# Two passes over each weight block: sixteen matmuls on the rounded weights, then sixteen on their rests

## The chip, the cores and the metric

The kernel runs on one core of a Trainium2 chip. The metric is the device time of that core in microseconds (us): 3598.67 us, the median of 3 runs (3596.43 to 3601.0). TensorE is the matmul engine; its granted clock is 1.2 or 2.4 GHz (0.50 or 1.00 in the profile's shares). VectorE (DVE) and ScalarE (ACT) do the elementwise work, SyncE (SP) issues the DMAs that bring the weights, GpSimd (POOL) does almost nothing.

## The reference, cut to what matters

The model is four layers on 256 tokens of width 2048, in float32: a windowed attention layer and a gated linear recurrence layer, each followed by a convolutional feed-forward part, and then an "even" and an "odd" attention layer. Almost all the work is dense projections of this kind:

```python
def conv_ffn(h, w_up, conv_w, conv_b, w_down):
    u = causal_dwconv(h @ w_up, conv_w, conv_b)
    g, v = jnp.split(u, 2, axis=-1)
    return (jax.nn.gelu(g, approximate=True) * v) @ w_down

# first_block: for layer in range(2):
#     x = x + sliding_window_attention(rmsnorm(x, ...), w_qkv, ..., w_o)   (layer 0)
#     x = x + rglru_block(rmsnorm(x, ...), w_in, ..., w_out)               (layer 1)
#     x = x + conv_ffn(rmsnorm(x, ...), w_up, ..., w_down)                 (D_FF = 6144)
# then an even layer (grouped-query heads with rotary positions, then differential heads)
# and an odd layer (16 dilated-window heads), each: x = x + (gated heads) @ w_out
```

## The kernel before, in words

Everything is kept transposed: features on the 128 partitions, the 256 tokens along the free axis. A *block* (a "unit" in the code) is one tile of 128 output features: its weights are 16 k-tiles of 128x128, held in one slot of 128x2048. There are 540 blocks, streamed in a fixed order of phases (table PHASES): `attn` 24 (the QKV projection), `wo` 16, three rounds of `up` 32 and `down` 16, `lru_y` 16, `lru_x` 32 (16 of them small gate blocks), `lru_out` 16, three more rounds of `up` and `down`, `even_kv` 4, `even_a` 16, `even_b` 32, `even_out` 16, `odd` 64, `odd_out` 16.

The float32 product is split in two float32r parts. ScalarE rounds the raw weights (`w_head`, L561), VectorE subtracts to get the rest (`w_tail`, L837). Activations are split the same way and stand side by side, 256 rounded columns and 256 of rests, in `h` (layer input) or `act` (input of the second product). For each k-tile TensorE runs one 128x512 matmul of `w_head` on both halves (L272) and one 128x256 matmul of `w_tail` on the rounded half (L273). All 32 matmuls of a block add up in one PSUM bank: columns 0 to 255 hold head times rounded plus tail times rounded, columns 256 to 511 head times rests. Two banks alternate.

Each engine has its own written order, joined by semaphores. For a block ScalarE first rounds the weights of the block three ahead (L561), then copies columns 256 to 511 (`lo`, L567) once `unit_done` says that the last matmul is through; VectorE adds columns 0 to 255 to it (`prod`, L843), scales it, makes the rest of the weights three ahead (L837) and does the phase's own work. TensorE may start a block when its weights are split (`tail_done`) and the bank of two blocks ago is read (`bank_free`).

Two arguments of `unit` put waits inside a block. `ready` is given to the first block of a phase whose input is just being made: before k-tile 0 it waits for the first 14 input tiles, before k-tile 14 for the fifteenth and before k-tile 15 for the last. `middle` is a list of small pieces issued after k-tile 8 (k == KT // 2): in the projection the column sums of a head's norm (`head_norm`, L289), in `even_kv` and `even_a` also rotations (`rotate`, L297), transposes of values (`turn_v`, L307), scores (L315), transposes of probabilities (`turn_p`, L326) and values (L335); in `even_b` and `odd` scores after k-tile 8 of the first block of four, `turn_p` in the third and the values in the fourth. Each piece begins with its own wait, and TensorE works strictly in order behind it. After the first block of a normed phase stands `token_norm` (L283), which waits for the sum of squares (`acc_done`). The very first block (`first_unit`, L373, L374) and the gate blocks (`gate_unit`, L430 to L432: twelve 128x256 matmuls in a row, each with its own weights) are written apart.

Of the kernel before, what the change touches and what calls it, by code (L numbers as in the profile page):

```python
# [29 lines left out]
P = 128  # L30
D_MODEL, SEQ = 2048, 256
KT = D_MODEL // P
# [53 lines left out]
def known(v):  # L86
    return isinstance(v, int)
# [30 lines left out]
def build(nc, t):  # L118

    ctx = ExitStack()  # L120
    with ctx:
        def sb(name, shape, dt=F32):
            return ctx.enter_context(nc.sbuf_tensor(name, shape, dt))
# [9 lines left out]
        w_tail = sb("w_tail", [P, RING, D_MODEL], F32R)  # L133
# [125 lines left out]
        def _(pe):  # L259
            def unit(u, slot, src, middle=(), ready=None):  # L260

                bank = unit_bank[slot % 2]
                pe.wait_ge(tail_done, u + 1)
                if not known(u) or u >= 2:
                    pe.wait_ge(bank_free, u - 1)
                for k in range(KT):
                    if ready and k in (0, KT - 2, KT - 1):
                        pe.wait_ge(ready[0], ready[1] - (2 if k == 0 else KT - 1 - k))  # L270
                    at = slice(k * P, (k + 1) * P)
                    pe.matmul(bank[:, :], w_head[:, slot, at], src[:, k, :], start=k == 0, stop=False)  # L272
                    last = pe.matmul(bank[:, 0:SEQ], w_tail[:, slot, at], src[:, k, 0:SEQ],  # L273
                                     start=False, stop=k == KT - 1)
                    if k == KT // 2:
                        for part in middle:
                            part()
                last.then_inc(unit_done, 1)

            def token_norm(n):  # L280
# [58 lines left out]
            def plain(name, src, ready=None, norm=None):  # L339

                def body(i):
                    for j in range(RING):
                        first = known(i) and j == 0
                        unit(i * RING + (BASE[name] + j), j, src, ready=ready if first else None)
                        if first and norm is not None:
                            token_norm(norm)
                repeat(pe, 0, UNITS[name] // RING, body)
# [40 lines left out]
            def project(i):  # L388
                for j in range(RING):
                    g = i * RING + j  # L390
                    if known(g) and g == 0:
                        first_unit()
                    else:
                        unit(i * RING + (BASE["attn"] + j), j, h, (trailing(i * RING + (j - 1)),))
# [41 lines left out]
            for j in range(2):  # L436
                unit(b + j, j, h)
# [23 lines left out]
            for i in range(A_HEADS // 2 + 1):  # L461

                n, last = 2 * i - 2, i == A_HEADS // 2
# [920 lines left out]
```

## Time and profile before

| | |
|---|---|
| median of 3 runs | 3598.67 us |
| profiled execution, device time | 3606.35 us |
| its span, first to last instruction | 3604.6 us |
| mean granted TensorE clock | 0.943 |
| TensorE matmul (PE) busy | 3336.0 us, 93% |
| TensorE weight load (PEld) busy | 2820.0 us, 78% |
| VectorE busy | 2456.4 us, 68% |
| ScalarE busy | 1789.5 us, 50% |
| head matmuls L272 | 5808 on `h`, 2560 on `act` |
| tail matmuls L273 | 5808 on `h`, 2560 on `act` |

The profile is of one execution, and durations below are its own. Matmuls overlap in the pipeline: a single one is shown with 0.40 or 0.28 us although the next starts earlier, so what a matmul costs is read from the distance between two starts. A bracket at the end of a row gives the idle time of that engine ahead of the instruction and who ended it. The chain of waits is followed backwards from the last instruction.

### The profile page before, as it was taken

What the parts mean: (1) busy time and instruction counts of PE and PEld (TensorE: products, weight loads), DVE (VectorE), ACT (ScalarE), POOL (GpSimd) and SP (SyncE); (2) the same over time, 40 slices, a digit from 0 to 9 for tenths busy, and PEclk for the clock granted to TensorE, in tenths of its full rate; (3) what the DMA queues carried; (4) which work ended last, traced back from release to release, by engine and by line L of the source; (5) the groups of instructions that cost most, each with busy time, mean ns of one, the idle gap of its engine ahead of it and who ended that gap; (6) DMA issues with size and microseconds to landing.
All of it is one profiled execution on the core that took longest, in us unless ns stands there. A gap on an engine that the chain in (4) does not pass through costs nothing.

```text
span 3604.6 us, 52426 instructions
## 1 busy us (share of the span) xinstructions
PE 3336.0 (93%) x17960; PEld 2820.0 (78%) x17960; DVE 2456.4 (68%) x3703; ACT 1789.5 (50%) x2281; POOL 13.1 (0%) x20
## 2 busy tenths in 40 slices
PE   8878999999999999769999999999778989999997
PEld 6744788888888888658888888888666777888876
DVE  6654577667667766777875775776455776666665
ACT  6843355445445445664554554554444554444443
POOL 1000000000000000000000000000000000000000
PEclk9965899999999999879999999999888999999998
DMA  5410355555555554235555555555223444445443
GB/s 186 144 43 0 105 186 187 181 187 184 182 187 186 182 180 150 95 117 176 197 186 187 186 179 186 185 184 186 105 84 105 152 149 141 174 164 175 173 146 122
DMA packets 83038, 561.11 MB, mean 156 GB/s; under 512 B 9728, under 2 KB 12800, under 8 KB 15872
## 3 DMA queue, kind: packets, MB, share of 16 engines
q1 hardware_dynamic: 82944, 559.87, 44.7%
q8 instruction: 57, 0.93, 0.1%
q14 instruction: 37, 0.30, 0.0%
HBM read 557.73 MB, written 2.10 MB: 155 GB/s over the span
## 4 chain that ended last, share of the span: by engine, by line
PE 70%; DVE 14%; issue 6%; ACT 6%; DMA 3%; DVEq 1%; ACTq 0%; SPq 0%
PE unit L272 42%; PE unit L273 21%; DVE w_tail L837 5%; PE o L335 2%; PE s L315 2%; PE tr L326 1%; DVE prod L843 1%; ACT w_head L561 1%; ACT L576 1%; DMA raw<-in_down 1%; ACT lo L567 1%; DMA raw<-in_lru_x 1%; ACT prt L613 1%; DVE mx L885 1%; DVE x L1024 0%
## 5 line engine op out<-in xcount | busy, mean ns | idle before, releaser
L272 PE MATMUL unit<-h,w_head 128*128 128x512 f32 x5808 | 2108.4, 406 | 40.1 <-DVE kv L1100 33.7
L273 PE MATMUL unit<-h,w_tail 128*128 128x256 f32 x5808 | 1643.3, 283 | 0.0
L272 PEld LDWEIGHTS unit<-h,w_head 128*128 128x128 f32 x5808 | 1110.9, 191 | 319.3 <-DVE kv L1100 37.0
L561 ACT ACTIVATE w_head<-raw 128x2048 fp32r<-128x2048 f32 (+1 forms) x540 | 1013.5, 1877 | 611.3 <-DMA raw<-in_up 210.8
L837 DVE TENSOR_TENSOR w_tail<-raw,w_head 128x2048 fp32r<-128x2048 f32 (+1 forms) x540 | 1209.5, 2240 | 11.5
L273 PEld LDWEIGHTS unit<-h,w_tail 128*128 128x128 f32 x5808 | 1115.4, 192 | 3.0
L272 PE MATMUL unit<-act,w_head 128*128 128x512 f32 x2560 | 910.7, 400 | 19.1 <-DVE act L854 12.9
L843 DVE TENSOR_TENSOR prod<-unit,lo 128x256 f32<-128x256 f32 x524 | 222.3, 424 | 756.2 <-ACT lo L567 750.4
L273 PE MATMUL unit<-act,w_tail 128*128 128x256 f32 x2560 | 720.6, 281 | 0.0
L272 PEld LDWEIGHTS unit<-act,w_head 128*128 128x128 f32 x2560 | 485.2, 190 | 140.6 <-DVE act L854 15.2
L273 PEld LDWEIGHTS unit<-act,w_tail 128*128 128x128 f32 x2560 | 487.7, 190 | 0.2
L567 ACT ACTIVATE lo<-unit 128x256 f32<-128x256 f32 x524 | 197.2, 376 | 316.2 <-PE unit L273 315.8
L691 ACT ACTIVATE kv<-kv,fconv 128x256 f32<-128x256 f32 x192 | 115.8, 603 | 187.3 <-DVE kv L849 187.3
L1045 DVE SCALAR_TENSOR_TENSOR kv<-kv,fconv 128x255 f32<-128x255 f32 (+1 forms) x384 | 184.8, 481 | 24.8 <-DVE kv L1045 0.9
L613 ACT ACTIVATE prt<-tr 128x512 f32<-128x512 f32 x64 | 38.3, 598 | 188.3 <-PE tr L326 188.3
L326 PE MATMUL tr<-ident,pr 128*128 128x128 f32 x256 | 59.4, 375 | 54.1 <-DVE pr L900 35.8
L607 ACT ACTIVATE pr<-pr,nm 128x256 f32<-128x256 f32 x144 | 71.5, 498 | 74.5 <-DVE nm L887 74.5
L849 DVE SCALAR_TENSOR_TENSOR kv<-prod,rstd 128x256 f32<-128x256 f32 x232 | 98.6, 425 | 9.0
L326 PEld LDWEIGHTS tr<-ident,pr 128*128 128x128 f32 x256 | 39.4, 188 | 82.5 <-DVE pr L900 41.5
L335 PE MATMUL o<-prt,kv 128*64 128x256 f32 (+1 forms) x160 | 72.3, 601 | 23.4 <-ACT prt L613 23.4
L587 ACT ACTIVATE sq<-x 128x256 f32 (+1 forms) x96 | 40.3, 419 | 107.9 <-DVE x L1024 107.9
L315 PE MATMUL s<-kv,store 64*128 64x256 f32 (+1 forms) x160 | 73.8, 622 | 9.9 <-DVE store L986 5.2
(157 smaller groups left out, 1610.4 us busy)
## 6 DMA issues: line engine op xcount, KB each, us to landing
raw<-in_up SPq DMA_DIRECT2D x192, 1024.0 KB, 4.9
raw<-in_down SPq DMA_DIRECT2D x96, 1024.0 KB, 4.9
raw<-in_odd SPq DMA_DIRECT2D x64, 1024.0 KB, 4.9
raw<-in_even_b SPq DMA_DIRECT2D x32, 1024.0 KB, 4.9
raw<-in_attn SPq DMA_DIRECT2D x24, 1024.0 KB, 4.9
raw<-in_wo SPq DMA_DIRECT2D x16, 1024.0 KB, 4.9
raw<-in_lru_y SPq DMA_DIRECT2D x16, 1024.0 KB, 4.9
raw<-in_lru_x SPq DMA_DIRECT2D x16, 1024.0 KB, 4.9
```

The source lines that it names most:

```text
L272: pe.matmul(bank[:, :], w_head[:, slot, at], src[:, k, :], start=k == 0, stop=False)
L273: last = pe.matmul(bank[:, 0:SEQ], w_tail[:, slot, at], src[:, k, 0:SEQ], start=False, stop=k == KT - 1)
L315: last = pe.matmul(bank[:, qt * SEQ:(qt + 1) * SEQ], q[:, qt * P:(qt + 1) * P], k, start=True, stop=True)
L326: last = pe.transpose(ps_t[:, kt * SEQ + qt * P:kt * SEQ + (qt + 1) * P], pr[:, slot, qt * SEQ + kt * P:qt * SEQ + (kt + 1) * P], ident[:, :])
L335: last = pe.matmul(out, v[kt], prt[:, kt * SEQ:(kt + 1) * SEQ], start=kt == 0, stop=kt == QT - 1)
L561: a.activation(w_head[:, slot, 0:width], raw[:, r, 0:width], ACT.Copy).then_inc(head_done, 1)
L567: a.activation(lo[:, slot % 2, :], unit_bank[slot % 2][:, SEQ:2 * SEQ], ACT.Copy).then_inc(lo_done, 1)
L691: a.activation(kv[:, 1 + j, :], kv[:, 0, :], ACT.Identity, scale=fconv[:, layer, tap, 2:3], bias=fconv[:, layer, tap, 3:4])\
L837: v.tensor_tensor(w_tail[:, slot, 0:width], raw[:, slot % 2, 0:width], w_head[:, slot, 0:width].bitcast(F32), ALU.subtract).then_inc(tail_ ...
L843: v.tensor_tensor(prod[:, :], unit_bank[slot % 2][:, 0:SEQ], lo[:, slot % 2, :], ALU.add)\
L849: return v.scalar_tensor_tensor(dst, prod[:, :], scale, rstd[:, :], ALU.mult, ALU.mult)
L1045: ins = v.scalar_tensor_tensor(y[:, back_by:SEQ], kv[:, 0, 0:SEQ - back_by], w, y[:, back_by:SEQ], ALU.mult, ALU.add)
```

## The change

The loop over the 16 k-tiles is split in two. The first loop issues the 16 head matmuls, with the waits of `ready` and the pieces of `middle` at the same k-tiles as before; a second loop issues the 16 tail matmuls. The first matmul of a block still clears the bank, the last tail still closes the sum and signals `unit_done`. `first_unit` and `gate_unit` are not touched.

```diff
@@ -270,11 +270,12 @@
                         pe.wait_ge(ready[0], ready[1] - (2 if k == 0 else KT - 1 - k))
                     at = slice(k * P, (k + 1) * P)
                     pe.matmul(bank[:, :], w_head[:, slot, at], src[:, k, :], start=k == 0, stop=False)
-                    last = pe.matmul(bank[:, 0:SEQ], w_tail[:, slot, at], src[:, k, 0:SEQ],
-                                     start=False, stop=k == KT - 1)
                     if k == KT // 2:
                         for part in middle:
                             part()
+                for k in range(KT):
+                    last = pe.matmul(bank[:, 0:SEQ], w_tail[:, slot, k * P:(k + 1) * P], src[:, k, 0:SEQ],
+                                     start=False, stop=k == KT - 1)
                 last.then_inc(unit_done, 1)
```

TensorE's order at the end of the first block of a `down` phase, before. The waits on `act_done` are those for the last two tiles of `act`:

```order
L272 MATMUL unit<-act,w_head 128x512
L273 MATMUL unit<-act,w_tail 128x256
L272 MATMUL unit<-act,w_head 128x512 [waits act_done]
L273 MATMUL unit<-act,w_tail 128x256
L272 MATMUL unit<-act,w_head 128x512 [waits act_done]
L273 MATMUL unit<-act,w_tail 128x256
L272 MATMUL unit<-act,w_head 128x512 [waits bank_free,tail_done]
```

The same block after the change, from its first matmul to the next block's:

```order
L272 MATMUL unit<-act,w_head 128x512 [waits act_done,bank_free,tail_done]
L272 MATMUL unit<-act,w_head 128x512 x13
L272 MATMUL unit<-act,w_head 128x512 [waits act_done] x2
L277 MATMUL unit<-act,w_tail 128x256 x16
L272 MATMUL unit<-act,w_head 128x512 [waits bank_free,tail_done]
```

Ahead of the last wait stood 15 heads and 15 tails, and now 15 heads; behind it stood one head and one tail, and now one head and 16 tails.

TensorE's order around k-tile 8 of the fourth block of a group in `even_a`, before (`o` is a head's values, `v` the rotation of the second query head):

```order
L272 MATMUL unit<-h,w_head 128x512
L273 MATMUL unit<-h,w_tail 128x256
L335 MATMUL o<-prt,kv 128x256 [waits o_read,pt_done]
L335 MATMUL o<-prt,kv 128x256
L297 MATMUL v<-store 128x256 [waits vt_done,q_done,rot_in]
L272 MATMUL unit<-h,w_head 128x512
L273 MATMUL unit<-h,w_tail 128x256
```

And the whole block after the change:

```order
L272 MATMUL unit<-h,w_head 128x512 [waits bank_free,tail_done]
L272 MATMUL unit<-h,w_head 128x512 x8
L336 MATMUL o<-prt,kv 128x256 [waits o_read,pt_done]
L336 MATMUL o<-prt,kv 128x256
L298 MATMUL v<-store 128x256 [waits vt_done,q_done,rot_in]
L272 MATMUL unit<-h,w_head 128x512 x7
L277 MATMUL unit<-h,w_tail 128x256 x16
```

The pieces stood after nine heads and nine tails, and now after nine heads; behind them stood seven heads and seven tails, and now seven heads and 16 tails.

## Rows read from the trace of the kernel before

**Rows 1.** The page, parts 1, 4 and 5: busy time, chain, costliest groups.

```profile
PE 3336.0 (93%) x17960; PEld 2820.0 (78%) x17960; DVE 2456.4 (68%) x3703; ACT 1789.5 (50%) x2281; POOL 13.1 (0%) x20
...
PE 70%; DVE 14%; issue 6%; ACT 6%; DMA 3%; DVEq 1%; ACTq 0%; SPq 0%
...
L272 PE MATMUL unit<-act,w_head 128*128 128x512 f32 x2560 | 910.7, 400 | 19.1 <-DVE act L854 12.9
```

**Rows 2.** Stretches: length, then busy us and instructions of each engine, clock, DMA.

```profile
670.00:930.00 260.00, 260.00 (x1474) 225.42 (x1473) 185.09 (x244) 128.56 (x137) 0.00 (x0) 1.00 0.53 185
1700.00:1870.00 170.00, 170.00 (x983) 148.59 (x982) 139.47 (x204) 97.61 (x112) 0.00 (x0) 1.00 0.55 191
```

**Rows 3.** Timeline, TensorE, first down phase: start, length, instruction, idle before.

```profile
666.88 0.28 PE L273 MATMUL unit<-act,w_tail 128*128 128x256 f32 x1
668.03 0.50 PE L272 MATMUL unit<-act,w_head 128*128 128x512 f32 x1 [0.88 <-DVE act L854]
```

**Rows 4.** Timeline, TensorE, first block of lru_y and its norm.

```profile
1302.83 0.50 PE L272 MATMUL unit<-h,w_head 128*128 128x512 f32 x1 [0.74 <-DVE h L860]
...
1305.36 1.22 PE L283 MATMUL norm<-acc,ones 128*128 128x256 f32 x2 [1.92 <-DVE acc L869]
```

**Rows 5.** Timeline, TensorE, a gate block: matmuls, and a weight load.

```profile
1465.19 0.28 PE L430 MATMUL unit<-act,w_head 128*128 x1
1465.31 0.28 PE L431 MATMUL unit<-act,w_head 128*128 x1
...
1465.19 0.19 PEld L431 LDWEIGHTS unit<-act,w_head 128*128 128x128 f32 x1
```

**Rows 6.** Timeline, TensorE, a down phase, slow rhythm.

```profile
1000.71 0.40 PE L272 MATMUL unit<-act,w_head 128*128 128x512 f32 x1
1000.95 0.28 PE L273 MATMUL unit<-act,w_tail 128*128 128x256 f32 x1
1001.07 0.40 PE L272 MATMUL unit<-act,w_head 128*128 128x512 f32 x1
```

**Rows 7.** Timeline, TensorE, an up phase, fast rhythm.

```profile
1750.04 0.27 PE L273 MATMUL unit<-h,w_tail 128*128 128x256 f32 x1
1750.15 0.40 PE L272 MATMUL unit<-h,w_head 128*128 128x512 f32 x1
1750.38 0.28 PE L273 MATMUL unit<-h,w_tail 128*128 128x256 f32 x1
```

**Rows 8.** A stretch and the timeline, TensorE and ScalarE, end of an even_a block.

```profile
2637.20:2641.80 4.60, 4.60 (x16) 3.83 (x15) 0.85 (x3) 0.00 (x0) 0.00 (x0) 0.50 0.07 25
...
2641.34 0.63 PE L272 MATMUL unit<-h,w_head 128*128 128x512 f32 x1
2641.77 0.41 PE L273 MATMUL unit<-h,w_tail 128*128 128x256 f32 x1
...
2642.22 0.38 ACT L567 ACTIVATE lo<-unit 128x256 f32<-128x256 f32 x1 [8.99 <-PE unit L273]
```

**Rows 9.** Timeline, start of even_out, and VectorE's last act tile.

```profile
2986.08 0.99 PE L272 MATMUL unit<-act,w_head 128*128 128x512 f32 x1
...
2991.41 0.43 DVE L854 TENSOR_TENSOR act<-store,act 128x256 fp32r<-128x256 f32 x1
```

**Rows 10.** Timeline, projection: next block's first matmul, and ScalarE's copy.

```profile
134.31 0.40 PE L272 MATMUL unit<-h,w_head 128*128 128x512 f32 x1
...
136.53 0.36 ACT L567 ACTIVATE lo<-unit 128x256 f32<-128x256 f32 x1
```

**Rows 11.** Timeline, TensorE, even_b, third block of four.

```profile
2872.11 0.65 PE L326 MATMUL tr<-ident,pr 128*128 128x128 f32 x4 [1.42 <-DVE pr L914]
```

**Rows 12.** Timeline, VectorE and TensorE, odd, third block of four.

```profile
3192.77 0.62 DVE L900 TENSOR_SCALAR pr<-pr,rd 128x256 f32<-128x256 f32 x2
...
3194.62 0.60 PE L326 MATMUL tr<-ident,pr 128*128 128x128 f32 x4
```

**Rows 13.** Line L567 from 2520 to 2740: who ended ScalarE's idle time.

```profile
  PE unit L273: 45.7, 8
```

## The prediction

> **What bounds the kernel now.** I read the page first: TensorE is busy 93% of the span, and the chain that ended last lies 70% on it and 14% on VectorE [rows 1]. Then the stretches of the span. In the feed-forward stages TensorE never stops and the granted clock is 1.00 (2.4 GHz): 260 us hold 1474 matmuls, which is 737 pairs of one 512-column matmul on a rounded block (head) and one 256-column matmul on its rest (tail), so 352.8 ns a pair; another stretch of 170 us holds 983 matmuls, 491.5 pairs, 345.9 ns each [rows 2]. So the same code runs at two rhythms. Of the 385 blocks that nothing interrupts 303 go in the slow rhythm and 82 in the fast one (counted by the starts of their first matmuls), a mean of 351.3 ns a pair. 432 of the 523 blocks that the change touches stand in stages bound by this rhythm (288 feed-forward, 80 of the five other plain stages of 16 [wo, lru_y, lru_out, even_out, odd_out], 64 odd attention): 6912 pairs, so 1 ns a pair is 6.9 us of the kernel.
>
> Then the waits, since the change moves the places in a block where TensorE waits. There are three kinds. (a) The first block of a phase waits for the last activation tile before k-tile 15: TensorE stood from 666.88 to 668.03 [rows 3], and the page charges 12.9 us of such waiting to the tile's writer on the line of the act blocks [rows 1]. (b) The first block of a normed phase waits the same way and is then followed by a norm matmul that waits for the sum [rows 4]. (c) In the attention stages small work is issued after k-tile 8 and waits for VectorE or ScalarE.
>
> **The change part by part.** It removes nothing and adds nothing: 16 head and 16 tail matmuls with their 32 weight loads stand in each block as before; only their order differs. No DMA, no other engine and no semaphore changes. What moves is what is late.
>
> *The rhythm.* In a run of heads and a run of tails each kind follows itself. Tails have a row: in the gate blocks 256-column matmuls follow each other, each with its own weights, at 0.12 us [rows 5]; in the alternation a head starts 0.11 or 0.12 after a tail [rows 6, 7]. Heads after heads have no row. A tail starts 0.23 to 0.24 us after a head [rows 6, 7], and that is the nearest I have for the time that a head holds the array: 241 ns at most. Below, the fast rhythm less a 120 ns tail leaves 226 ns, and, farther off, half of the 0.43 us that a head takes at the lower clock (0.50 granted, 1.2 GHz) is 213 ns [rows 8]. So a pair in two passes costs 226 + 120 = 346 to 241 + 120 = 361 ns, against 351.3. The tail's 120 is measured, four more than the 116 it has in the slow rhythm. If the cost above the columns' own time belongs to each matmul and its load and is only booked on the neighbour, the order does not matter. I take that, 352 ns, a change of 0; the ends are -5.3 x 6.9 = -37 us and +9.7 x 6.9 = +67 us.
>
> The Trainium skill, "TensorE: Matmul & The Clock Gate", section "Back-to-back issue gap", gives N/2.4 + 2.5 ns as the isolated gap of a matmul of N columns at full clock. That would be 216 + 109 = 325 ns a pair in either order; the trace shows 346 to 353 [rows 2], so the rule lacks some 20 to 28 ns here and cannot say whose they are. By it the rhythm term would be 0, as an estimate, if the excess stays, and far below 0 if alternation makes it.
>
> *The last tile of a phase.* Before, 15 heads and 15 tails are done when TensorE waits for the last act tile, and after it one head and one tail remain. Now only the heads are done, and 15 tails more remain: 15 x 0.12 = 1.8 us later at each such place. The wait only starts earlier, since VectorE makes the tile from the last up block, whose end does not move. There are seven such places, the six down phases and lru_out (of the 12.9 us the six take 0.88 each [rows 3], the rest is lru_out's). At that one the lower clock makes the tails 0.21 us each at first, but the clock would rise no later than before, so in the end only columns at full clock are lost: 1.8. Sum 7 x 1.8 = 12.6 us, all on the path, since TensorE is the bound behind it. The other boundaries are free: at wo and odd_out the tile comes early in the block, and even_out's is there at 2991.84, 5.8 us after the block's start, while fifteen heads at the lower clock need up to 15 x 0.43 = 6.4 [rows 9].
>
> *Normed phases.* The last h tile came at 1302.83 and the norm matmul could start at 1305.36 [rows 4]. The two-pass block needs 0.24 + 16 x 0.12 = 2.16 us from there and ends at 1304.99: hidden, 0.37 us to spare. The same at the five such places. If that cover went, each would cost up to 1.8 us.
>
> *Work after k-tile 8.* Its place moves from 9 pairs (3.2 us) into the block to 9 heads (2.1 us); behind it stand 7 heads and 16 tails instead of 7 pairs: 9 x 0.12 = 1.08 us more. Where TensorE waits there for another engine, the block's end moves by that much against the work after k-tile 8. It costs only if somebody waits for that end.
> - QKV projection: the block ends at 134.31 and ScalarE takes it up at 136.53, because it makes roots and rounds weights until then [rows 10]. 2.2 us of cover against 1.08: 0. Its entry may shift by some 0.7.
> - Differential attention (even_b): the turn of the probabilities waits for VectorE [rows 11]; the block ends 1.6 us or more before ScalarE comes for it. 0. Its first scores can come up to 0.7 earlier, which cancels the entry above.
> - Odd attention: VectorE ends the probabilities at 3193.39, TensorE turns them at 3194.62 without a wait [rows 12]. This place would move 1.08 earlier against the block's end, and 1.23 of slack takes it: 0. If that failed, 16 x 1 us.
> - even_kv and even_a: eight times ScalarE stood idle until the block's last matmul, 45.7 us in all [rows 13]. One of them: last tail issued at 2641.77, ScalarE takes the block up at 2642.22 [rows 8]. Each of the eight costs 9 tails, 1.08 us at full clock, 9 x 0.21 = 1.9 where the lower clock lasts. Together 8.6 to 15; I take 10, since the low stretch usually ends within a microsecond of the block's end.
>
> **Sum:** 12.6 + 10 + 0 = +22.6 us on the profiled execution's 3606.35 us (span 3604.6): 3629. That execution stands 7.7 us above the median of the runs, 3598.67, so the median would be 3621.3. What a measurement can tell from no change is 0.2%, 7.2 us.
>
> **Rivals.**
> 1. *Runs of one kind go faster, and the kernel with them* (the other side). A load starts together with the matmul before it (1465.19 for both [rows 5]), so each head covers its successor's load twice over. If heads in a row then take 226 ns, a pair is 346 and the rhythm gives -37 against +22.6: 3584. It decides from a pair of 348.0 ns down (22.6 / 6.9 = 3.3 under 351.3). For it: the fast rhythm exists, unexplained, for the same instructions. Against: the gate blocks' tails are at the slow end of the tail intervals. Its extreme, 213 + 120 = 333, gives 3598.7 + 22.6 - 126 = 3495.
> 2. *Short after short is bound by the weight load.* In alternation a tail's slot was 112 to 117 at times, in its own run always 120; if heads keep the slow rhythm's 237, a pair is 357: +5.7 x 6.9 = +39, in all 3660; with 241, 3688. For it: [rows 5] against [rows 7]. Against: the 4 ns may be the head's, booked one matmul later.
> 3. *The moved waits cost nothing and the rhythm stays:* each later end is caught up by slack that I read as none: 3600. Against it: after such a wait TensorE has no idle time for 260 us in which 1.8 us could be won back [rows 2].
>
> The Trainium skill, same page, Part 2 step 1 ("Step-by-step"), says that the queue pulls weight loads ahead of running matmuls, so with two loads ahead one long matmul could shelter both its neighbour's and the next, which the two-pass order would lose. The trace shows a load never starting before the matmul ahead of it (1465.19 for both [rows 5]), so only one load is ahead and no shelter is lost; with two ahead it would come out as rival 2.
>
> **How the numbers follow.** Forecast case (waits as summed, rhythm within 2 ns): 0.47, 3607 to 3640. Rival 1: 0.24 (its extreme 0.03 of it). Rival 2: 0.19. Rival 3: 0.10. The time is the likeliest case's, 3621. The range goes down to rival 1's 3584 with a little room and up into rival 2, 3576 to 3662; its own range for the forecast case is 3607 to 3640. Faster by over 0.2%: rival 1 without its border cases, 0.22. Within 0.2%: most of rival 3 and rival 1's border, 0.11. Slower: 0.67.
>
> **What would show it.** Right: the head to head interval near 0.23 and the tail to tail near 0.12 in the feed-forward stages, 16 of each in 5.63 us; at a down phase the last act tile followed by one head and 16 tails, 2.2 us; the norm matmul of a normed phase still waiting for its sum, not for the block; eight blocks of even_kv and even_a ending 1.1 to 1.9 us later after their middle work. Wrong: a count of pairs in 260 us other than about 737; TensorE waiting in the odd attention at the turn of the probabilities; or ScalarE's wait for block ends turning up in the projection.

## The result and the profile after

The two-pass kernel takes 3614.82 us (median of 7 runs, 3609.33 to 3621.56) where the kernel before took 3599.32 us in its 7 (3596.43 to 3607.44). The ratio of the runs is 1.004, with a 95% interval of 1.0028 to 1.0052: 0.4% slower, 15 us. The forecast was 3621, slower.

The page of the two-pass kernel, parts 1, 4 and 5; columns as in [rows 1]:

```profile
PE 3330.3 (92%) x17960; PEld 2846.2 (79%) x17960; DVE 2454.5 (68%) x3703; ACT 1786.0 (49%) x2281; POOL 13.1 (0%) x20
...
PE 72%; DVE 12%; issue 6%; ACT 6%; DMA 3%; DVEq 1%; ACTq 0%; SPq 0%
...
L272 PE MATMUL unit<-act,w_head 128*128 128x512 f32 x2560 | 626.6, 397 | 32.0 <-DVE act L855 25.8
```

As many instructions as before, and the idle time that the last act tiles end has doubled, from 12.9 to 25.8 us. The stretches answer to [rows 2]; two lie inside feed-forward stages, the third behind the first of those waits:

```profile
1890.00:2140.00 250.00, 250.00 (x1439) 220.97 (x1439) 178.96 (x236) 123.95 (x134) 0.00 (x0) 1.00 0.54 188
1710.00:1870.00 160.00, 160.00 (x918) 141.23 (x918) 131.87 (x190) 90.42 (x105) 0.00 (x0) 1.00 0.55 190
670.10:674.00 3.90, 3.90 (x17) 3.81 (x18) 0.00 (x0) 0.00 (x0) 0.00 (x0) 0.50 0.40 170
```

250 us hold 719.5 pairs, 347.5 ns each, and the fast stretch of before is slightly slower now, 348.6. A stretch cuts its first and last block (this one holds 464 heads and 454 tails), so whole phases are the better measure: the 512 pairs of up01 take 178.13 us, 347.9 ns each, where they took 180.91, 353.3 ns, in the slow rhythm and 177.49, 346.7 ns, in the fast one (in e5 below). There is one rhythm: of the 380 blocks that nothing interrupts 376 take 5.57 us from end to end, where before 303 took 5.65 and 82 took 5.55. So where TensorE is bound by its own work the new order is faster than the slow rhythm, and slightly slower than the fast one. The third stretch shows the clock at 0.50. TensorE's timeline at the same place as [rows 3], where equal matmuls in a row are drawn together (x15, x16):

```profile
661.75 2.08 PE L277 MATMUL unit<-h,w_tail 128*128 128x256 f32 x16
663.66 3.59 PE L272 MATMUL unit<-act,w_head 128*128 128x512 f32 x15
670.01 0.79 PE L272 MATMUL unit<-act,w_head 128*128 128x512 f32 x1 [2.76 <-DVE act L855]
670.60 3.62 PE L277 MATMUL unit<-act,w_tail 128*128 128x256 f32 x16
674.02 2.27 PE L272 MATMUL unit<-act,w_head 128*128 128x512 f32 x5
```

The last act tile comes 6.35 us after the block began, as before (6.34). TensorE waits 2.76 us for it instead of 0.88, and behind it stand one head and 16 tails, which at 1.2 GHz take 4.0 us (670.01 to 674.02) where 2.16 was forecast and a pair took 0.47 before.

The boundary of lru_y, answering to [rows 4]:

```profile
1310.04 0.50 PE L272 MATMUL unit<-h,w_head 128*128 128x512 f32 x1 [1.89 <-DVE h L861]
1310.38 3.14 PE L277 MATMUL unit<-h,w_tail 128*128 128x256 f32 x16
1313.32 1.05 PE L284 MATMUL norm<-acc,ones 128*128 128x256 f32 x2
```

The norm matmul no longer waits for its sum (no bracket): it waits for the block's own tails. It starts 3.28 us after the last h tile, 2.53 before, and the clock is low for most of the way (the stretch: busy us and matmuls of TensorE, clock, DMA):

```profile
1310.40:1313.30 2.90, 2.90 (x17) 0.60 0.26 110
```

And the idle time of ScalarE that a block's last matmul ends, from 2520 to 2760, which holds the same 20 blocks as [rows 13]:

```profile
  PE unit L277: 54.1, 10
```

The span by phases, in us, each phase from the sum (`prod`) of the last block of the phase ahead of it to its own (read from the traces of this kernel, of the one before and of four experiments told below):

| phases | before | two passes | e1 | e3 | e4 | e8 |
|---|---|---|---|---|---|---|
| attn and wo | 481.1 | 484.6 | 481.9 | 480.3 | 482.1 | 484.2 |
| up01, up02, up11, up12, each | 180.9 | 178.1 | 178.3 | 178.2 | 178.1 | 178.1 |
| down00, 01, 10, 11, mean | 91.6 | 93.9 | 90.3 | 90.3 | 92.1 | 95.1 |
| down02 and down12 | 187.8 | 195.7 | 188.2 | 188.3 | 192.3 | 198.5 |
| up00, lru_y and up10 | 452.5 | 448.8 | 446.4 | 447.9 | 448.7 | 454.9 |
| lru_x and lru_out | 299.8 | 300.9 | 299.3 | 299.6 | 301.7 | 303.8 |
| even_kv and even_a | 223.5 | 232.0 | 233.3 | 223.6 | 231.2 | 243.5 |
| even_b to the end | 869.7 | 869.8 | 867.4 | 866.5 | 866.8 | 869.3 |
| span | 3604.6 | 3619.8 | 3590.8 | 3580.1 | 3603.8 | 3647.2 |

The four up phases that have no boundary with a wait win 2.8 us each. The six down phases lose 17 us net, 25 against the rhythm (16 blocks win 1.4 us in each), and the two even phases lose 8.5.

### The profile page after: what moved, and what is told of

Same layout as the page of the kernel before. It is cut to its first block, busy times and chain, and to the rows that moved or that the text cites. A ratio compares the mean times of both kernels' runs of the same rounds, so it can differ in the third digit from the quotient of the medians.

```text
span 3619.8 us, 52426 instructions
## 1 busy us (share of the span) xinstructions
PE 3330.3 (92%) x17960; PEld 2846.2 (79%) x17960; DVE 2454.5 (68%) x3703; ACT 1786.0 (49%) x2281; POOL 13.1 (0%) x20
## 4 chain that ended last, share of the span: by engine, by line
PE 72%; DVE 12%; issue 6%; ACT 6%; DMA 3%; DVEq 1%; ACTq 0%; SPq 0%
PE unit L272 42%; PE unit L277 23%; DVE w_tail L838 4%; PE o L336 2%; PE s L316 2%; PE tr L327 2%; DVE prod L844 1%; ACT L577 1%; ACT w_head L562 1%; ACT lo L568 1%; DMA raw<-in_lru_x 1%; ACT prt L614 1%; DMA raw<-in_wo 1%; DMA raw<-in_down 1%; DVE x L1025 0%
## 5 line engine op out<-in xcount | busy, mean ns | idle before, releaser
L272 PE MATMUL unit<-h,w_head 128*128 128x512 f32 x5808 | 1470.6, 403 | 44.1 <-DVE kv L1101 30.9
L272 PEld LDWEIGHTS unit<-h,w_head 128*128 128x128 f32 x5808 | 1094.7, 193 | 267.3 <-DVE kv L1101 33.5
L838 DVE TENSOR_TENSOR w_tail<-raw,w_head 128x2048 fp32r<-128x2048 f32 (+1 forms) x540 | 1209.4, 2240 | 11.5
L277 PEld LDWEIGHTS unit<-h,w_tail 128*128 128x128 f32 x5808 | 754.3, 193 | 30.8
L277 PE MATMUL unit<-h,w_tail 128*128 128x256 f32 x5808 | 761.1, 284 | 0.0
L272 PE MATMUL unit<-act,w_head 128*128 128x512 f32 x2560 | 626.6, 397 | 32.0 <-DVE act L855 25.8
L277 PEld LDWEIGHTS unit<-act,w_tail 128*128 128x128 f32 x2560 | 335.8, 195 | 12.4
L277 PE MATMUL unit<-act,w_tail 128*128 128x256 f32 x2560 | 339.5, 287 | 0.0
```

The lines of the kernel that those rows point to most:

```text
L277: last = pe.matmul(bank[:, 0:SEQ], w_tail[:, slot, k * P:(k + 1) * P], src[:, k, 0:SEQ], start=False, stop=k == KT - 1)
L838: v.tensor_tensor(w_tail[:, slot, 0:width], raw[:, slot % 2, 0:width], w_head[:, slot, 0:width].bitcast(F32), ALU.subtract).then_inc(tail_ ...
```

## The experiments

All of these are edits of the two-pass kernel's loop in `unit`, but e5. The diffs are shortened at the dots, and their comments are added here. The ratios are to runs of the kernel before that were taken together with them: medians 3596.68 (29 runs, for e1 to e4) and 3598.28 us (23 runs, for e5 to e8). The cuts in e1, e2, e3, e6 and e7 are the k-tiles at which a run of heads ends and their tails follow.

**e1, the first block of each phase back in the alternating order.**

```diff
-for k in range(KT):
+cuts = list(range(1, KT + 1)) if ready else [KT]
+k0 = 0
+for k1 in cuts:
+    for k in range(k0, k1):
...
         pe.matmul(bank[:, :], w_head[:, slot, k * P:(k + 1) * P], src[:, k, :], start=k == 0, stop=False)
...
+    for k in range(k0, k1):
         last = pe.matmul(bank[:, 0:SEQ], w_tail[:, slot, k * P:(k + 1) * P], src[:, k, 0:SEQ],
                          start=False, stop=k == KT - 1)
+    k0 = k1
```

> The two-pass kernel, with only the first block of each phase (those with the ready waits) back in the alternating order. Theory A: the loss at the phase boundaries is made by the 15 tails left behind the last wait and by the clock that falls to 1.20 GHz in the longer idle time ahead of it; in the two profiles the six down phases lost 25 us against the rhythm they keep elsewhere, lru_out 3. All of it comes back: about 3587 us, with 3573 to 3595 as its range. Rival B: only the 15 tails (7 x 1.8 = 12.6 us) hang on the order, the slow clock in the down phases on something else: about 3602 us. Rival C: the loss is made inside all blocks: no change, 3615.

Measured: 3593.26 us, ratio to before 0.9988 (0.9977 to 1.0). The first blocks of 19 phases, of 523 blocks in all, hold more than the whole loss. Against the two-pass profile the four plain down phases go from 93.9 to 90.3, and the clock keeps 1.00 there; lru_out is 2.0 us shorter, up00 and lru_y 1.2 each. The time is in theory A's range, 6 us above its 3587; the 3602 of rival B (the 15 tails alone) lies above the interval, which ends at 3597. The two ratios, 1.004 and 0.9988, put what came back at 0.5%, 19 us (13 to 25).

**e2, the blocks with work after k-tile 8 back in the alternating order.**

```diff
+cuts = list(range(1, KT + 1)) if middle else [KT]
```

> The two-pass kernel, with only the blocks that carry work after k-tile 8 back in the alternating order. Theory A: even_kv and even_a give back the 8.5 us they lost, the projection up to its 3.9, and odd loses 48 blocks x 0.05 = 2.4 us of rhythm: about 3605 us. Rival: the longer rest behind that work is hidden and the even stages lost time for another reason: 3617 or more.

Measured: 3604.02 us, 1.0009 (0.9996 to 1.0022), 11 us under the two-pass kernel. Theory A had 3605, the rival 3617 or more. In its profile even_kv and even_a take 223.6 us, as before the change (223.5), and attn and wo 482.1 against 484.6. One term was a miss: odd was to lose 2.4 us of rhythm and took 394.3, 1.9 less than in the two-pass profile.

**e4, filler matmuls ahead of the last wait of the down phases.**

```diff
+if k == KT - 1 and ready and ready[1] in (32, 48, 64, 96, 112, 128) and ready[0] is act_done:
+    for f in range(KT - 1):
+        pe.matmul(ps_s0[:, 0:SEQ], w_tail[:, slot, f * P:(f + 1) * P], src[:, f, 0:SEQ], start=True, stop=True)
```

> The two-pass kernel with 15 filler matmuls of 256 columns (their sums go to a bank that nobody reads) ahead of the last wait of each of the six down phases, so that TensorE is busy there as long as it was before the change, while 16 tails still stand behind the wait. Theory A (idle time ahead of the wait makes the clock fall): the low clock in the down phases goes, each boundary loses only its 15 tails, 1.8 us instead of 4.2 on the mean, so about 14 us come back: 3600 us. Rival B (the clock falls for another reason): no change, 3615. Rival E (the filler itself delays the block): over 3615.

Measured: 3608.44 us, 1.0025 (1.0014 to 1.0036), 0.15% or 5 us under the two-pass kernel, less than the 14 expected from its profile. The intervals of the two kernels overlap, so the time alone does not decide between theory A and rival B; the profile does. The first down boundary of e4, TensorE's timeline (L271 is the filler):

```profile
661.08 3.59 PE L276 MATMUL unit<-act,w_head 128*128 128x512 f32 x15
664.51 1.95 PE L271 MATMUL s<-act,w_tail 128*128 128x256 f32 x15
667.43 0.50 PE L276 MATMUL unit<-act,w_head 128*128 128x512 f32 x1 [0.97 <-DVE act L859]
667.76 2.08 PE L281 MATMUL unit<-act,w_tail 128*128 128x256 f32 x16
669.68 2.68 PE L276 MATMUL unit<-act,w_head 128*128 128x512 f32 x11
```

Same wait, same 16 tails behind it; only the idle time is 0.97 instead of 2.76 us. The clock now stays at 1.00, and head and tails take 2.25 us (667.43 to 669.68) instead of 4.01. In all four plain down phases e4 takes 92.1 us, 0.5 over before, which is +1.9 for the tails and -1.4 for the rhythm. So the first term has two parts, shown apart: 1.9 us from the tails, and what the clock takes. The clock's part varies: 94.8, 94.9, 93.6 and 92.15 us in the two-pass profile, the last one with no low clock at all. The profile of e2, whose down phases are those of the two-pass kernel, has 93.6, 92.1, 93.7 and 94.9, and again the one of 92.1 is the only one without the low clock. In the two-pass kernel's timeline, the same wait is followed by head and tails in 2.25 us:

```profile
2155.30 0.50 PE L272 MATMUL unit<-act,w_head 128*128 128x512 f32 x1 [2.77 <-DVE act L855]
2155.63 2.08 PE L277 MATMUL unit<-act,w_tail 128*128 128x256 f32 x16
2157.55 3.85 PE L272 MATMUL unit<-act,w_head 128*128 128x512 f32 x16
```

Over all runs the mean granted clock goes up too, from 0.935 to 0.938 (medians). Why the median time gained less than the profiles compared (16 us) is not shown; the profiled execution of the two-pass kernel was the slowest of its seven, 7 us above their median.

**e3, two passes cut where a block waits.**

```diff
+cuts = [KT - 1, KT] if ready else [KT // 2 + 1, KT] if middle else [KT]
...
+    if k1 == KT // 2 + 1:       # behind the tails of this cut
+        for part in middle:
+            part()
```

> Two passes everywhere, but cut where a block waits: the first block of a phase runs 15 heads, 15 tails, then the last head and tail; blocks with work after k-tile 8 run 9 heads, 9 tails, the work, 7 heads, 7 tails. Theory A (the gain is a quicker rhythm of runs, 348 ns a pair against 351.3; the loss is what stands behind the waits): all losses of e1 and e2 come back and the rhythm is kept, about 3575 us, 3568 to 3585. Rival D (the rhythm gains only in whole passes of 16): the cut blocks give it up, 3580 to 3590. Rival C: no better than before, 3599.

Measured: 3585.27 us (3581.93 to 3586.38), 0.996 (0.9945 to 0.9975): faster than both kernels. The same boundary in e3:

```profile
659.62 3.59 PE L274 MATMUL unit<-act,w_head 128*128 128x512 f32 x15
663.05 1.95 PE L279 MATMUL unit<-act,w_tail 128*128 128x256 f32 x15
665.97 0.50 PE L274 MATMUL unit<-act,w_head 128*128 128x512 f32 x1 [0.97 <-DVE act L861]
666.30 0.28 PE L279 MATMUL unit<-act,w_tail 128*128 128x256 f32 x1
```

15 tails stand ahead of the wait again and one behind it, and the blocks keep 5.57 us (354 of 385). It is above the 3575 expected, just outside theory A's range and inside rival D's (the cut blocks give the rhythm up). Against D: odd, where 45 of the 64 blocks carry such work and are cut at it, takes 395.3 us, and 396.2 in whole passes. What is smaller than expected is the gain against before, 0.4% in the medians and 24.5 us between the two profiles; the profiled execution of before was 8 us above its median, that of e3 3 us below. In the profiles the phases with waits are as before (the even ones 223.6 against 223.5), so I read e3 against before as the rhythm, -0.4% or 14 us (9 to 20), and the two-pass kernel against e3 as the price of the waits: 1.004 / 0.996 = 1.008, 29 us (22 to 36). e1 and e2 agree: what they gave back is 19 and 11 us.

**e5, the kernel before once more.** No edit.

> The kernel before, unchanged, for a second profile. Theory G (each stretch of the alternating order falls into one of two rhythms, 352.8 or 345.9 ns a pair, by how its first matmuls happen to meet the clock): the count of pairs per stretch differs from the first profile in some stretches, always near one of the two values, and the time moves with it by up to 20 us. Theory H (the rhythm is set by the place in the program): the same stretches are fast as in the first profile.

Measured: 3600.41 us, one run. Stretches of before, then of e5 (columns: busy us and matmuls of TensorE, clock, DMA):

```profile
520.00:650.00 130.00, 130.00 (x738) 1.00 0.54 186
700.00:850.00 150.00, 150.00 (x851) 1.00 0.53 184
1700.00:1850.00 150.00, 150.00 (x868) 1.00 0.55 191
1890.00:2140.00 250.00, 250.00 (x1417) 1.00 0.54 187
```

```profile
520.00:650.00 130.00, 130.00 (x738) 1.00 0.54 186
700.00:850.00 150.00, 150.00 (x868) 1.00 0.54 189
1700.00:1850.00 150.00, 150.00 (x851) 1.00 0.53 185
1890.00:2140.00 250.00, 250.00 (x1444) 1.00 0.54 189
```

The same instructions give 851 matmuls in one execution and 868 in the other, in exchange between two stretches, and the fourth differs too. Theory G, in that the alternating order has two rhythms and the choice differs between executions. In these two profiles a rhythm, once begun, holds until TensorE waits or other matmuls stand between the blocks (in odd it changes there without any wait). What makes the choice was not looked into. It moves the time: 114 blocks were fast in e5, 82 in the first profile, which at 0.10 us each is 3 of the 6 us between their spans (3598.6 and 3604.6). Whether the spread of the runs comes from it is open: it is 3589 to 3611 us in the 29 runs of before and 3582 to 3586 in the 6 of e3, but 3590 to 3608 in the 12 of e7 below, which has one rhythm.

**e6 and e7, groups of two and of four k-tiles.**

```diff
+cuts = list(range(2, KT + 1, 2))     # e6
+cuts = list(range(4, KT + 1, 4))     # e7
```

> All blocks in groups of two k-tiles: two heads, two tails, and so on; the waits stay at their k-tiles. Theory G1 (only strict alternation has the slow rhythm): a block takes 5.57 us as in two passes, in all stretches alike; behind the last wait of a phase stand one head and two tails, so almost nothing is lost there: 3583 to 3588 us. Theory S (each change between head and tail costs): 16 changes instead of 2 or 32, a block of about 5.60 us: 3592 us.

> All blocks in groups of four k-tiles. Behind the last wait of a phase stand one head and four tails (three tails more than before, 0.36 us at seven places), behind the work after k-tile 8 seven heads and eight tails. Theory G1: blocks of 5.57 us and 3 us lost at the boundaries: 3585 to 3590 us. Theory S: 8 changes a block, 5.58 us: the same time, told apart by the length of a block.

Measured: e6 3590.77 us, 0.9975 (0.9963 to 0.9987); e7 3602.96 us, 1.0007 (0.9995 to 1.0019). The stretch from 1900 to 2100 (columns as in e5), of before, of the two-pass kernel, of e6 and of e7:

```profile
1900.00:2100.00 200.00, 200.00 (x1134) 1.00 0.54 187
```

```profile
1900.00:2100.00 200.00, 200.00 (x1152) 1.00 0.54 188
```

```profile
1900.00:2100.00 200.00, 200.00 (x1150) 1.00 0.54 188
```

```profile
1900.00:2100.00 200.00, 200.00 (x1142) 1.00 0.53 186
```

That is 352.7, 347.2, 347.8 and 350.3 ns a pair; by the length of the up phases (180.91, 178.13, 178.35 and 179.63 us) 353.3, 347.9, 348.3 and 350.8. e6 has the blocks of 5.57 us that theory G1 wanted, but its time is above G1's range and near theory S's 3592; in its profile attn and wo take 5 us and the two even phases 3.4 us longer than in e3, which the expectation did not count. Both theories fail on e7, which was to take 3585 to 3590. A price for each change between head and tail would put it between e6 and two passes, and a slow rhythm of strict alternation alone would put it beside them; it has a rhythm of its own (5.61 us a block in 353 of 384). In these profiles each order has its own fixed pattern of intervals, and only alternation has two; e6 and e7 have one profile each. What makes the patterns was not found.

**e8, the pass of tails first.**

```diff
 for k in range(KT):
...
+    if k == 0:
+        pe.matmul(bank[:, :], w_head[:, slot, at], src[:, k, :], start=True, stop=False)
+    pe.matmul(bank[:, 0:SEQ], w_tail[:, slot, at], src[:, k, 0:SEQ], start=False, stop=False)
...
+for k in range(1, KT):
+    last = pe.matmul(bank[:, :], w_head[:, slot, k * P:(k + 1) * P], src[:, k, :],
+                     start=False, stop=k == KT - 1)
```

> The passes the other way round: head 0, then the 16 tails, then heads 1 to 15; the waits of the ready and middle arguments stand in the pass of tails. The dose of the suspected cost: behind the last wait of a phase stand a tail and 15 heads (3.5 us at full clock instead of 2.2), the idle time ahead of it grows by 1.6 us, and behind the work after k-tile 8 stand 7 tails and 15 heads (4.3 us instead of 3.5 and 2.5). Theory A: each of the seven boundaries costs 1.5 us or more over the two-pass kernel, even_kv and even_a 6 to 12 us more, and odd loses the slack of 1.2 us at the turn of the probabilities, up to 1 us in each of 15 rounds: 3640 us, 3630 to 3660. Rival C (the losses have nothing to do with what stands behind the waits): as the two-pass kernel, 3615.

Measured: 3649.19 us, 1.0143 (1.0123 to 1.0164). Its first down boundary:

```profile
671.06 0.39 PE L274 MATMUL unit<-act,w_tail 128*128 128x256 f32 x1 [4.17 <-DVE act L857]
671.28 5.19 PE L279 MATMUL unit<-act,w_head 128*128 128x512 f32 x15
676.30 0.39 PE L273 MATMUL unit<-act,w_head 128*128 128x512 f32 x1
```

5.24 us from the last tile to the next block, after 4.17 us idle. The time is in theory A's range, 3630 to 3660. even_kv and even_a lose 20 us against before and 11.5 against two passes (6 to 12 expected); each plain down phase loses 3.5 against before and 1.2 against two passes, a little under the 1.5 expected. But odd loses nothing (395.9 us; before 396.8). There the slack was expected to break. TensorE's turn and VectorE's last piece ahead of it, in e8:

```profile
3264.36 0.61 PE L329 MATMUL tr<-ident,pr 128*128 128x128 f32 x4
```

```profile
3263.57 0.61 DVE L903 TENSOR_SCALAR pr<-pr,rd 128x256 f32<-128x256 f32 x2
```

VectorE ends at 3264.18, 0.18 us ahead: the wait stays just covered, here and in all but one of the 15 rounds (0.7 us of waiting there). In the two-pass profile the same place, answering to [rows 12], is

```profile
3209.34 0.62 DVE L901 TENSOR_SCALAR pr<-pr,rd 128x256 f32<-128x256 f32 x2
```

```profile
3210.94 0.60 PE L327 MATMUL tr<-ident,pr 128*128 128x128 f32 x4
```

with 0.98 us of slack, where 1.23 less 1.08 would have left 0.15. The scores that start this chain stand after k-tile 8 too and moved with its end: from them to the turn it is 11.5 us before, 11.4 in two passes and 11.3 in e8. In e8 VectorE's last piece comes later behind the scores, which takes most of the slack.

## Why the prediction was right, and where it was not

The direction and the mechanism were right, the time was 6 us off, and the range held it. That the time came so close is luck in part, since two errors of opposite sign met in the sum: the waits were priced at +22.6 us and cost 29 (1.004 / 0.996; 22 to 36), and the rhythm was put at 0 and gave 0.4%, 14 us (9 to 20).

*The rhythm* (taken: 352 ns a pair, a change of 0). Mis-sized. 347.2 to 347.9 was measured, close to the low end of 346. Runs of tails take 120 ns each, as the gate blocks showed [rows 5]; runs of heads take 227 (median of the starts), the 226 of the lower bound and not the 232 taken. The remark that the cost might only be booked on the neighbour was nearly right for the fast rhythm: 345.9 there, 347 now. What I missed is that the slow rhythm, 353, goes with strict alternation (no other order here has it) and is not in the same stretches in each execution. One profile could not show that.

*The last tile of a phase* (7 x 1.8 us). The place, the 15 tails and the arrival of the tile were right (6.35 and 6.34 us into the block), and 1.9 us each is what e4 shows. Missing was the clock: of these places the text considered it for lru_out alone, where it was low already, and not that 2.76 us of idle time instead of 0.88 can make it fall in the down phases. The six cost 25 us in the two-pass profile where 10.8 was forecast; lru_out is 2.0 us longer than in e1, for 1.8 forecast.

*Normed phases* (hidden, 0.37 us to spare). Right at the full clock, wrong at the low one, where the cover of 2.5 us is too short: 3.28 us passed at lru_y instead of 2.53. In the two-pass profile up00 and lru_y, where the clock fell, took 179.7 and 90.6 us, against 178.5 and 89.4 in e1; up10, where it stayed at 1.00, took 178.5 in both, and so did up00 in e2. In the order of before the clock could fall there too, behind the norm's own wait (0.50 from 1306 to 1310 in the first profile), but the norm matmul was out by then.

*Work after k-tile 8.* Right in mechanism and size. Eight block ends were named in even_kv and even_a and 10 us taken; 8.5 was measured, and e2 and e3 give back just that. Ten ends are waited for now, eight before. The projection was forecast at 0. Its phase was 3.9 us longer in the profile, but e5, with the code of before, was 2.5 longer, so nothing can be said there. even_b: 0 forecast, +1.2, and about as much in the profiles of e1 to e4; the cause is open. Odd: no cost, right, but not for the reason given: the slack was not used up, because start and end of the chain moved together (e8).

*The rivals.* Rival 1 was right on the rhythm (347 against 346) and wrong on the end. Its threshold of 348.0 was passed, and yet the kernel is slower, for two reasons: the waits cost more than 22.6, and in the medians the rhythm gave 14 us, 2 ns a pair, where the one profile of before promised 3.4 to 4.1. Its load covered "twice over" is not in the rows: a load is shown with 0.19 us and a head with 0.23 to 0.24. Rival 2 did not happen: the tails' 120 ns came with shorter heads. Rival 3 is excluded by e1, e2 and e8. The Trainium skill's formula, 325 ns a pair ("TensorE: Matmul & The Clock Gate", "Back-to-back issue gap"), is met by none of the four orders, which take 346 to 353. That no load starts before the matmul ahead of it holds for all loads of the blocks; the exceptions, 27 of 17960, are loads of scores on 64 rows that run side by side.

## What to carry to other kernels

In an engine that works in order, count what stands between a wait and the next thing that others wait for: a reorder that changes no work changes that, and what was moved behind a wait is paid in full where nothing covers it, as in the down phases (1.9 us each), and not at all where something does, as in odd. Fill the time ahead of a wait with work that does not need it: idle time there can cost a second time, in the clock, and so ought to be in the sum. Cut a pass at its waits and keep its order elsewhere; e3, cut at k-tile 15 and after k-tile 8, kept the gain, and its phases with waits take what they took before.

## What the runs showed of the hardware

- The order of 512-column and 256-column float32r matmuls, each with its own weight load, changes the time of a pair at the granted clock of 1.00: 347.2 ns in runs of 16, 347.8 in twos, 350.3 in fours, and 345.9 or 352.8 in strict alternation (by counts in stretches; by whole phases each is 0.5 to 0.8 more). At 1.2 GHz a pair took 640 ns in every order; half of that would be 320.
- Strict alternation takes one of its two rhythms for a whole stretch between waits or other matmuls, and can take the other one there in the next execution: 82 fast blocks in one profile, 114 in another. As an estimate, all of some 385 plain blocks at 0.10 us each would be 38 us, 1% of the kernel.
- The wait of 2.8 us at the start of a down phase was followed by the low clock in three of the four plain down phases of the two-pass execution, and in three of the four in e2's; with 0.97 us idle (e3, e4) it never was there. A plain down phase took 92.1 us where the clock stayed and 93.6 to 94.9 where it fell.
